# Loading and summing the second column pair of an up projection earlier, and moving one copy ahead of a gelu

## What is computed

```python
mixed = jnp.concatenate([attn, ssm], axis=-1) @ w_out[l]
x = x + gate1 * rms_norm(mixed, post_mix_w[l])

h = rms_norm(x, pre_ffn_w[l]) * (1.0 + scale2) + shift2
u = causal_dwconv(h @ w_up[l], ffn_conv_w[l], ffn_conv_b[l])   # 3 taps
u_gate, u_val = jnp.split(u, 2, axis=-1)
f = (jax.nn.gelu(u_gate, approximate=True) * u_val) @ w_down[l]
```

## Time and profile before

| | |
|---|---|
| time, median of 3 runs | 1139.71 us (1139.21 to 1140.12) |
| the profiled execution: its own time | 1136.96 us |
| its span, first to last instruction | 1135.0 us |
| mean granted TensorE clock | 0.985 |
| PE busy | 1080.2 us (95%) |
| DVE busy | 867.8 us (76%) |
| ACT busy | 560.8 us (49%) |
| POOL busy | 250.1 us (22%) |

### The profile page before, as it was taken

How to read it: one execution, slowest core, us unless ns; L and a number is a source line. 1 busy time by engine, 2 the same in 40 slices (tenths; PEclk the granted TensorE clock), 3 DMA queues, 4 the chain that set the end, 5 groups by cost and what they waited for, 6 DMA issues and landing times.

```text
span 1135.0 us, 14878 instructions
## 1 busy us (share of the span) xinstructions
PE 1080.2 (95%) x5096; PEld 868.2 (77%) x5096; DVE 867.8 (76%) x1121; ACT 560.8 (49%) x1012; POOL 250.1 (22%) x237
## 2 busy tenths in 40 slices
PE   4699999999989999997999999999999999999997
PEld 4578766766767888765888888888888888888885
DVE  5869676767558688778888888888888877777687
ACT  4812254556464655665544444444444545454453
POOL 2000011111224442215333333333333100000012
PEclk9899999999999999998999999999999999999999
DMA  9989401001234222224343434343433595632324
GB/s 355 307 265 319 131 23 34 20 20 37 58 113 146 76 94 74 74 73 150 132 163 112 153 124 153 124 145 132 145 132 111 193 388 206 213 102 93 102 85 167
DMA packets 117487, 157.40 MB, mean 139 GB/s; under 512 B 15292, under 2 KB 76221, under 8 KB 117437
## 3 DMA queue, kind: packets, MB, share of 16 engines
q1 hardware_dynamic: 117117, 155.69, 40.9%
q0 software_dynamic: 320, 1.06, 0.3%
HBM read 125.75 MB, written 30.98 MB: 138 GB/s over the span
## 4 chain that ended last, share of the span: by engine, by line
PE 80%; DVE 9%; ACT 4%; DMA 3%; issue 2%; POOL 1%; SPq 1%; DVEq 0%; POOLq 0%; ACTq 0%
PE ps L2429 35%; PE ps L2099 18%; PE ps L2496 18%; DVE big L1387 3%; DMA raw<-in_w_in_dram 2%; PE ps L2138 2%; PE ps L2164 1%; PE ps L2152 1%; DMA scratch<-in_rel_bias_dram 1%; DVE big L1765 1%; DVE w_lo L1428 1%; PE ps L2269 1%; PE ps L2055 1%; PE ps L2368 1%; PE ps L2197 1%
## 5 line engine op out<-in xcount | busy, mean ns | idle before, releaser
L2099 PE MATMUL ps<-a_hi,w_hi 128*128 128x512 f32 x416 | 142.7, 422 | 7.5 <-DVE a_lo L1447 3.8
L2099 PE MATMUL ps<-a_lo,w_hi 128*128 128x512 f32 x416 | 132.6, 397 | 0.0
L2099 PE MATMUL ps<-a_hi,w_lo 128*128 128x512 f32 x416 | 131.8, 395 | 0.0
L2496 PE MATMUL ps<-w_hi,a_hi 128*128 128x512 f32 x308 | 119.9, 389 | 0.2 <-DVE a_lo L1931 0.2
L2496 PE MATMUL ps<-w_lo,a_hi 128*128 128x512 f32 x308 | 119.8, 389 | 0.0
L2496 PE MATMUL ps<-w_hi,a_lo 128*128 128x512 f32 x308 | 119.8, 389 | 0.0
L1299 ACT ACTIVATE w_hi<-raw 128x512 fp32r<-128x512 f32 x77 | 48.7, 632 | 98.3 <-PE ps L2496 87.6
L2099 PEld LDWEIGHTS ps<-a_hi,w_hi 128*128 128x128 f32 x416 | 73.3, 192 | 29.6 <-issue 16.3
L1219 ACT ACTIVATE scratch<-ps 128x512 f32<-128x512 f32 x88 | 52.3, 594 | 87.0 <-PE ps L2429 87.0
L2099 PEld LDWEIGHTS ps<-a_hi,w_lo 128*128 128x128 f32 x416 | 79.2, 190 | 18.2
L2099 PEld LDWEIGHTS ps<-a_lo,w_hi 128*128 128x128 f32 x416 | 79.5, 191 | 17.8
(11 more groups left out here) (267 smaller groups left out, 2394.0 us busy)
## 6 DMA issues: line engine op xcount, KB each, us to landing
big<-in_w_ada_dram SPq DMA_DIRECT2D x20, 1024.0 KB, 8.7
raw<-in_w_up_dram SPq DMA_DIRECT2D x22, 512.0 KB, 5.1
big<-in_w_up_dram SPq DMA_DIRECT2D x22, 512.0 KB, 5.1
big<-in_w_down_dram SPq DMA_DIRECT2D x22, 512.0 KB, 6.4
down_weight_sums<-big SPq DMA_DIRECT2D x22, 512.0 KB, 3.4
raw<-down_weight_sums SPq DMA_DIRECT2D x44, 256.0 KB, 2.8
ffn_hidden<-big SPq DMA_DIRECT2D x21, 512.0 KB, 2.6
big<-ffn_hidden SPq DMA_DIRECT2D x21, 512.0 KB, 8.4
```

What stands on the lines that cost most here:

```text
L2099: mm = pe.matmul(out, lhs_of[a], rhs_of(b, j), start=first and p == 0, stop=last and p == 2)
L2496: mm = pe.matmul(bk, a[:, ts], rhs_op(s)[w], start=fresh and m == 0, stop=last and m == 2, skip_group_check=s // KH in (J6, J3, J7))
```

## The change

SP no longer loads pair 1 into `raw_late` behind the token work. Before it waits for block 7's residual, it loads three pieces: `a21` of pair 1 into the third quarter of `raw`, `a22` into `normw`, and the gate rows into the first half of `raw`. It waits for pair 0's a1 split and pair 0's sums to be made, which frees these parts of `raw`, for the last reader of `normw`, and for the earlier load of pair 1's a1. POOL makes pair 1's sums from there, right behind block 7's last reciprocal root, without waiting for pair 0's lo parts (other buffers). The load of pair 2 now waits also for pair 1's sums. In ACT's list the copy of pair 1's first product stands ahead of pair 0's gelu instead of behind it.

```diff
@@ weight_source
-            if isinstance(p, int) and p == 1 and kind == "a1":
-                return scratch[:, 2048:3072]
+            if isinstance(p, int) and p == 1 and kind in ("a1", "a22"):
+                return scratch[:, 2048:3072] if kind == "a1" else normw[:, :]
@@ SP
             for b in range(NB):
                 if b + 3 < NB:
                     load_decay(b + 3)
+                if b == NB - 1:
+                    sp.wait_ge(s_ul, weights_to(0, "a1"))
+                    sp.wait_ge(s_us, 2)
+                    sp.wait_ge(s_my, NB)
+                    sp.wait_ge(s_a1, 16)
+                    sp.dma_start(raw_pair(0)[:, T:T + 512].rearrange("p (k n) -> p k n", k=4),
+                                 w_up2[0:512, P + FF:2 * P + FF].rearrange("(k p) n -> p k n", p=P))\
+                        .then_inc(s_uw[1], 16)
+                    sp.dma_start(normw[:, :].rearrange("p (k n) -> p k n", k=4),
+                                 w_up2[512:1024, P + FF:2 * P + FF].rearrange("(k p) n -> p k n", p=P))\
+                        .then_inc(s_a1, 16)
+                    sp.dma_start(raw_pair(0)[:, 0:T].rearrange("p (k n) -> p k n", k=KT),
+                                 w_up2[:, P:2 * P].rearrange("(k p) n -> p k n", p=P)).then_inc(s_uw[1], 16)
...
-            sp.wait_ge(s_tk, sums_to("t3", REST))
-            sp.wait_ge(s_bl, splits_to("b22", REST))
-            load_pair(1, 1)
-
@@ pair_traffic
-                    sp.wait_ge(s_us, p * 2 + 2)
+                    sp.wait_ge(s_us, 4 if first else p * 2 + 2)
                     load_pair(p + 2, par)
@@ POOL, weight_sums
-                raw_p, (one, two) = raw_pair(par), weight_sum(p)
+                raw_p = raw_pair(0 if isinstance(p, int) and p == 1 else par)
+                one, two = weight_sum(p)
                 a11, a12, a21, a22 = (raw_p[:, 512 * j:512 * j + 512] for j in range(4))
+                second = isinstance(p, int) and p == 1
+                if second:
+                    a22 = normw[:, :]
+                    pool.wait_ge(s_a1, 32)
                 pool.wait_ge(s_uw[par], (p // 2 + 1) * 32 if isinstance(p, int) else (p - par) * 16 + 32)
                 if not first:
-                    if isinstance(p, int):
+                    if second:
                         pool.wait_ge(s_mf, NB)
-                    pool.wait_ge(s_ul, weights_to(p - 1, "s12"))
+                    else:
+                        pool.wait_ge(s_ul, weights_to(p - 1, "s12"))
...
-                    if isinstance(p, int):
+                    if second:
                         pool.wait_ge(s_x1[1], 16 * NB // 2)
                         pool.wait_ge(s_n2, NB)
-                    pool.wait_ge(s_ul, weights_to(p - 1, "s34"))
+                    else:
+                        pool.wait_ge(s_ul, weights_to(p - 1, "s34"))
@@ ACT, weight_hi
-                if isinstance(p, int) and p == 1 and kind == "a1":
-                    act.wait_ge(s_a1, 16)
+                if isinstance(p, int) and p == 1 and kind in ("a1", "a22"):
+                    act.wait_ge(s_a1, 16 if kind == "a1" else 32)
@@ ACT, up_pair
                 copy_product(p - 1, 1 - par, 3, first=second)
+                if second:
+                    copy_product(p, par, 0)
                 weight_hi(p, par, "s34")
                 gelu(p - 1)
-                copy_product(p, par, 0)
+                if not second:
+                    copy_product(p, par, 0)
                 val_first_tap(p - 1, first=second)
```

More of the change, by code:

```diff
@@ L450, in hybrid_layer_kernel @@
         s_us, s_uq = sem("up_weight_sums"), sem("up_pool_chain")
-        s_a1 = sem("first_rows_of_pair_1_loaded")
+        s_a1 = sem("rows_of_pair_1_loaded_apart")
         s_uh, s_ul = sem("up_weights_hi"), sem("up_weights_lo")
```

## The result

The change makes the kernel faster: 1134.56 us against 1139.71 us, medians of 7 runs each, ratio 0.9949 with a 95% interval of 0.9931 to 0.9966. By this ratio the gain is 5.8 us (3.9 to 7.9); the two medians, whose quotient the ratio is not exactly, lie 5.15 us apart. The prediction said 1133.2 us, with 1130.2 to 1136.2 as its range. The profiled execution took 1133.78 us (span 1131.7) against 1136.96 (1135.0).

The account below looks back on a forecast made before the run. The DVE and ACT chain from the second assembly to pair 2's copy sets the seam; 7.84 shift + 1.41 slack - 2.75 for moved sums = 6.5 us, from 1139.7 to 1133.2 us, range 1130.2 to 1136.2.

Parts of the forecast that it names:

- main case: Whole change: gain 6.5 us to 1133.2 us, own range 1132 to 1134.3, no clock cost counted; chance 0.61.
- rival B: Clock falls in the new pause before pair 2's s2 times t2: 8 slow matmuls cost 1.6, gain 4.9 us; chance 0.16.
- The DVE and ACT chain sets the seam: From pair 1's second assembly to the copy of pair 2's first product: 25.85 us, unshortened by the change, sets the end.
- X: Start of DVE's second assembly, `assemble(0, 0, 1)`, at 516.89 before; forecast at 511.8 with the moved sums' price.
- Shift of X: Second assembly on DVE starts at 509.05 instead of 516.89, 7.84 us earlier, before the moved sums' price.
- The loads hidden: Pair 1's early loads land at 486 or so, before POOL is ready for them at 488.67.
- d: Delay of DVE's token work by POOL's moved additions taking turns: 2.75 us, bounds 0 and 5.1.
- Slack of 1.4 us: At pair 2's s2 times t2, PE was 1.41 us behind the end of its copy; this adds to the gain.
- Sum: Gain at the seam: 7.84 + 1.41 - 2.75 = 6.5 us.
- The pauses that I forecast: PE stands still some 1 us for pair 2's a1 and 2.6 us for the copy before its s2 times t2.
- rival D: PE stays at low clock through pair 0's five products: slower by 1.8 us, about 1141.5; chance 0.05.
- Rival A: POOL's moved additions don't hold DVE back: no price, gain 9.2 us, 1130.5 us; chance 0.12.

Follow-up runs that it names:

- experiment 1: The change with the copy of pair 1's first product put back behind pair 0's gelu; 1134.79 us, ratio 0.9954 to the kernel before.
- experiment 2: The kernel before with only the copy of pair 1's first product moved ahead of pair 0's gelu; 1139.16 us, ratio 0.9993 to the kernel before.
- experiment 6: The change with POOL's sums of pair 1 made to wait for the last token split; 1136.74 us, ratio 0.9962 to the kernel before.
- experiment 3: The change with pair 1's four POOL additions on 4 columns instead of 512 (tiny sums, output wrong); 1131.96 us, ratio 0.9926 to the kernel before.
- experiment 4: The change with the copy of each pair's first product ahead of the previous pair's gelu, in every pair; 1131.14 us, ratio 0.9920 to the kernel before.
- the repetition of 4: The change with the copy ahead of gelu in every pair, run once more beside the change; 1130.45 us, ratio 0.9912 to the kernel before.

## Why the prediction was right

The direction is right, and so is the sum up to s2 times t2 of pair 2. The whole gain is not the main case's, and part of the hit is luck: the median, 1134.56 us, lies outside the main case's own 1132 to 1134.3, and inside the stated range because that reached beyond rival B.

**The DVE and ACT chain sets the seam.** Right. X to the end of pair 2's copy took 25.90 us against 25.85 read before. The two halves of the change tell it best: the moved copy alone brings nothing (experiments 1 and 2), although it removes a 3.03 us pause. This length is no constant: in experiment 6 it is 27.08.

**Shift of X, 7.84 us without the sums' price.** 7.87 with tiny sums. **The loads hidden.** Right: the rows took 3.1 to 5.1 us to land and POOL's first sum follows the root without a wait.

**d, the price of the moved sums, 2.75 us.** 2.57 at the t2 sum, 2.58 at X by experiment 3. The play by turns fits instruction by instruction, and L1677 (now L1696), which no row before showed beside POOL, waits as the two-operand ones do: 1.76 instead of 0.75 us. That settles the price between 2.1 and 2.75. The Trainium skill, "SBUF — State Buffer", section "Who interferes with whom", says that a tensor_scalar in a two-port mode can contend with GpSimd. The trace agrees, with its 1.76 us; that L1696 runs in that mode is not shown as such, only that alone it takes 0.75 us where a tensor_tensor of the same size takes 1.22.

**Slack of 1.4 us.** 1.35 in experiment 2. **Sum.** 6.5 us forecast to s2 times t2 of pair 2, 6.60 measured. The pauses that I forecast, 1 and 2.6 us, came out as 0.26 and 2.26; the first is smaller because PE's clock had fallen behind the 3.14 us pause and made it later.

**Rival B, the clock.** This is the term that the main case put at nothing, and it came: 1.74 us in the profiled execution against 1.6 put down for B. B had a chance of 0.16 against the main case's 0.61. The sign that the prediction named for it, a granted clock near 0.5 after 537, stands in the windows above. The main case's reasons against it, a pause shorter than 3.03 us and the one of 1.57 that left no mark, did not carry: 2.26 us was enough here, though not each time (last section). Seam for seam the result is B's 4.9 us (measured 4.86), not the 6.5 forecast; the run times, 5.8 us in one series and 9.1 in the other, do not tell B from the main case. The fall behind the 3.14 us pause came too, as rival D began, but for 3 us and not for the whole of pair 0, and it is hidden: experiment 4 had no fall there and its repetition had one (0.50 from 499 to 501), and their seams differ by 0.01 us. **Rival A** (POOL doesn't hold DVE back) fell with the first DVE rows.

## What to carry to other kernels

Before a pause is priced at its length, follow what the next engine's list does to the point where it runs free: a pause can be removed and come back one pair later at the same cost. The copy of pair 1 ahead of the gelu was worth nothing by itself; the same move in every pair was worth 3.9 us on top of the change. Work that moves from an idle POOL to a place beside a busy DVE is paid in turns, about 1 us of DVE for each addition of 1.27 us, unless DVE reads an operand from PSUM or has a gap; it can still be the better place, and a tiny version of the work measures that price exactly. When run times scatter by more than the effect, compare profiles from a fixed point just ahead of the changed stretch: here that repeated to 0.02 us, in two kernels profiled twice each.

## What the runs showed of the hardware that was not expected

A PE pause of 2.26 or 2.27 us was followed by a fall to 1.2 GHz in four profiled executions (the change twice, experiments 2 and 3). Experiment 6 had two such pauses, at 534.00 and 544.72, and a fall behind neither, while the pause of 2.30 us at 516.04 in the same execution had one (0.50 from 516 to 519):

```profile
516.04 0.80 PE L2449 MATMUL ps<-a_hi,w_hi 128*128 128x512 f32 x1 [2.30 <-DVE w_lo L1748]
```

A pause of 3.13 or 3.14 us was followed by a fall in four (the change twice, experiment 1, the repetition of 4) and not in the fifth, experiment 4, whose windows are:

```profile
498.00:499.00 1.00, 0.38 (x2) 1.00 0.00 0
499.00:500.00 1.00, 1.00 (x6) 1.00 0.03 8
500.00:501.00 1.00, 1.00 (x6) 1.00 0.00 0
```

With the 3.03 us before and the 2.54 of experiment 1, 11 of the 14 pauses between 2.26 and 3.14 us at the seam had a fall behind them, and none of those of 1.57 us or less. So a pause of 2 to 3 us can cost another 1.6 to 1.7 us beyond its length, where PE's work behind it is what the rest waits for; behind the pause of 3.13 us, ahead of pair 0's products, the fall was hidden. What decides whether it falls is open.
